# Spreading the running maxima of four recurrent heads over the partitions: by DMAs that read one row 128 times in place of selector products and copies

## The chip, the cores and the metric

One core of one Trainium2 chip runs the whole program in one launch. The metric is device time in microseconds (us) of that core; before, three runs gave 3002.44, 3003.31 and 3006.01, median 3003.31. A core has five engines with their own instruction streams (TensorE or PE, VectorE or DVE, ScalarE or ACT, GpSimd or POOL, SyncE or SP) that meet only at semaphores, an on-chip memory of 128 partitions (SBUF), eight accumulator banks (PSUM) and 16 DMA engines. Here SP issues most loads, and ACT issues some.

## The reference, cut to what matters

The model runs two transformer layers over 512 tokens of width 1024 and then a second block, whose middle is a bidirectional gated recurrence (mLSTM) of 4 heads over 256 context and 512 latent tokens. The part that the change touches is the stabiliser of that recurrence. In the reference:

```
b = jnp.cumsum(jax.nn.log_sigmoid(f_pre).reshape(bsz, nh, nc, CHUNK), axis=-1)
dmat = jnp.where(mask, b[..., :, None] - b[..., None, :] + ip[..., None, :], -jnp.inf)
inter = b + m_in[..., None]
m_t = jnp.maximum(jnp.max(dmat, axis=-1), inter)
s = jnp.einsum('bhctk,bhcsk->bhcts', q, k) * jnp.exp(dmat - m_t[..., None])
```

The kernel doesn't work by chunk states. For a head h and a direction d it computes, for each block of 128 keys s, the weight exp(ip_s - b_s - M_t) for all 512 latent queries t, where M_t is the running maximum over keys of ip - b up to t. M is one row of 512 numbers for each (h, d). In the weights the keys lie on the partitions and the queries in the free dimension, so the row M must stand in all 128 partitions: that copy is `maximum(h, d)`, 128x512 numbers of fp32.

## The kernel before, in words

Every large product is made of three fp32r products (`mm3`, L454 to L457: high by high, low by high, high by low), each over a stationary 128x128 block and up to 512 columns. Weights come from DRAM in chunks of 512 KB (eight 128x128 blocks) into four stage slots, which SP loads in order (`load`, L2827: chunk i waits until chunk i-4 is split); ACT makes the high part (`weights`, L1233 to L1257), DVE the low part (L1888), and PE uses the chunk. The order of work on each engine is written out by hand, function by function; nothing is reordered at run time.

The part around the change, in PE's order:

- Gates: DVE makes the running sums and maxima of the eight gate rows by scans; row 32d+h of `T0[:, 256:768]` is M for (h, d). `gates_last` (L2472) ends with the semaphore name "scans". `SEL` is a constant of 36x1024 that SP loads into `TAB` (L2857): block 4d+h has ones in row 32d+h alone.
- The `pu` products (L1014 to L1027), eight steps k of four `mm3` each, two steps to a weight chunk; after k = 1 PE transposes the gates (`columns_of_gates`, L998), after k = 4 and 6 it runs `running_max(0, d)` (L1010): a product of the selector block and T0 into the bank `STAT`. ACT copies the bank to `maximum(0, d)` (L1713).
- `output_gate(3)` (its weights are the chunk after those of `pu`), then the pool means (`poolm` chunks, L1116), the first q and k, and the loop over the heads.
- The loop over h = 0..3 and over key blocks c = 0..5: PE makes the scores; ACT makes the exponents from `maximum(h, d)` (`exponents`, L1750; on the diagonal block DVE L2547 and ACT L1754); DVE multiplies (L2557); ACT takes the high part (L1276), POOL the low part (L2706); PE multiplies with the values and sums (`sums`, L1080 to L1082). `running_max(h+1, d)` stands in c = 2 and 3 of head h, on PE behind the scores of the next block and on ACT behind `weigh(h, c)`. At a head's end ACT runs `exponents(h+1, 0)` and then `denominators(h)` (L1769), for which PE's transposes (L1091) and DVE (L2565) wait; the normalisation of head h is done during head h+1.

Of the kernel before, what the change touches and what calls it, by code (L numbers as in the profile page):

```python
# [189 lines left out]

def program(nc, ws, wm, xT, cT, params, cond, consts, sel_d, out, plan):
    dry, chunks, upto = plan.dry, plan.chunks, plan.upto
    signals = {}
    ctx = ExitStack()
    with ctx:
        def signal(name, step=1):
            signals[name] = Signal(name, ctx.enter_context(nc.semaphore(f"s_{name}")), plan, step)
            return signals[name]
# [10 lines left out]
        landed = [signal(f"ws{i}", 16) for i in range(NS)]  # L209
        modl = [signal(f"md{i}", 16) for i in range(6)]  # L210
        x_in = [signal(f"x{t}", 16) for t in range(DT)]
        par_in, cond_in, idn_in, dft_in, c_in, rope_in, sel_in, mask_in, stored = (
# [30 lines left out]
        ROPE = [TAB[:, 896:1408], TAB[:, 1408:1920]]  # L243
        SEL = TAB[0:GATE_ROWS, 0:1024]
        TRI = [TAB[:, 1024:1152], TAB[:, 1152:1280]]
# [93 lines left out]
        def maximum(h, d):  # L339
            return Z[:, 4 + 2 * (h % 2) + d, :]  # L340

        def folded(g):


            a = 16 * S if g % 2 == 0 else 0
            return GHf[:, a:a + 514], GLf[:, a:a + 514]
# [70 lines left out]
        SCORE_OF = {n: name for name, n in SCORES.items()}  # L417
        def maximum_bank(h, d):

            return PS[2 * (h % 2) + d] if h else STAT  # L420


# [9 lines left out]
        def tensor(e):  # L432
# [568 lines left out]

            def running_max(h, d):
                if h == 0:
                    stat_free()
                elif h == 1:
                    banks.wait(pe, 2 + d)
                else:
                    pe.wait_ge(dv, "nrm", h - 2, d)
                a = (d * 4 + h) * 128
                done(e.matmul(maximum_bank(h, d)[:, :], SEL[:, a:a + 128], T0[:, 256:768], start=True, stop=True), ("mx", h, d))  # L1010
                if h == 0:
                    stat["free"] = (ev, ("mx", h, d))

            pu = [take_bank(("pu", c), lo, "pu", c) for c in range(4)]  # L1014
            for k in range(8):
                wh, wl = block(*[("w_in2", 0, k * 128, 1552 + q * 128) for q in range(4)])
                for c in range(4):
                    inst = mm3(pu[c][:, :], HH[:, k, c * 128:c * 128 + 128], HL[:, k, c * 128:c * 128 + 128], wh, wl, k == 0, k == 7)
                if k == 7:
                    ended(inst, ("pu",))  # L1020
                elif cur["used"] == 8:
                    ended(inst)
                if k == 1:
                    columns_of_gates()
                elif k in (4, 6):
                    pe.wait_ge(sel_in, "sel")
                    running_max(0, k // 2 - 2)  # L1027

# [34 lines left out]
            def sums(h, c):  # L1063
                if c == 0:
                    if h == 0:
                        for d in range(2):
                            banks.wait(pe, d)
                        pe.wait_ge(modv, "m", len(MODS) - 1)
                    else:

                        pe.wait_ge(lo, "qk", h, 0)
                        pe.wait_ge(ev, "mx", h, 1)
                        pe.wait_ge(ev, "den", h - 1)
                for d in range(2):
                    a, b = spans(c, d)
                    es = WEIGHED[h, c, d] % 4
                    eh, el = GH[:, 14 + es, 0:b - a], GL[:, 14 + es, 0:b - a]
                    va = GH[:, 6 + c, h * 128:h * 128 + 128], GL[:, 6 + c, h * 128:h * 128 + 128]
                    pe.wait_ge(plo, "e", h, c, d)
                    mm3(PS[2 * (h % 2) + d][:, a:b], *va, eh, el, c == 0, c == 5)  # L1080
                    e.matmul(DEN[0:2, a:b], ROW[:, d, :], eh, start=c == 0 and d == 0, stop=False, skip_group_check=True)
                    inst = e.matmul(DEN[0:2, a:b], ROW[:, d, :], el, start=False, stop=c == 5 and d == 1,  # L1082
                                    skip_group_check=True)
                    done(inst, ("sum", h, c, d))
# [83 lines left out]
            for h in range(NH):  # L1168
                more = h + 1 < NH
                for c in range(5):  # L1170
                    scores(h, c + 1)
                    if h == 0 and c == 1:
                        pool_out(3)
                    if c < 2 and h:
                        normalize(h - 1, c)
                    elif 2 <= c < 4 and more:
                        running_max(h + 1, c - 2)
                    if c >= 2 and not more:
                        early(*beside[2 * c - 4:2 * c - 2])
                    if c:  # L1180
                        sums(h, c - 1)
                    if c == 3 and h:
                        head_sums(h - 1)
                    elif c == 4 and h:
                        rms_last(("hn", h - 1), S, dv, "hn1", h - 1)
                if more:
                    pe.wait_ge(ev, "mx", h + 1, 0)
                    q_and_k(h + 1, 0, maximum_bank(h + 1, 0))
                else:
                    early(*beside[6:8])  # L1190
                sums(h, 4)
                if more:
                    q_and_k(h + 1, 1, score_bank("qk", h + 1, 1))
                    q_and_k(h + 1, 2, score_bank("qk", h + 1, 2))
                else:
                    early(*beside[8:10])
                sums(h, 5)
                if more:
                    scores(h + 1, 0)
                else:  # L1200
                    early(*beside[10:12])
                denominators(h)
# [26 lines left out]
        def scalar(e):  # L1229
# [471 lines left out]
            for c in range(2):  # L1701
                high(GH[:, 6 + c, :], bank("v2", c)[:, :], "v2", c)

            weights(("tr",))
            act.wait_ge(dv, "gct")
            act.wait_ge(mm, "tr")
            e.activation(GC[:, 6:10, :].rearrange("p a b -> p (a b)"), STAT[:, 216:360], ACT.Exp,
                         scale=-1.0).then_inc(ev.sem, ev.up(("fc",)))

            def running_max(h, d):  # L1710
                act.wait_ge(mm, "mx", h, d)
                act.wait_ge(padd, "out+", ("ao", 0, 0), 6)
                e.activation(maximum(h, d), maximum_bank(h, d)[:, :], ACT.Copy).then_inc(ev.sem, ev.up(("mx", h, d)))  # L1713

# [18 lines left out]
            def exponents(h, c):  # L1733
                for d in range(2):
# [10 lines left out]
                    if before:  # L1745
                        act.wait_ge(signals[before[0]], *before[1])
                    act.wait_ge(ev, "mx", h, d)
                    if rest.stop > rest.start:
# [46 lines left out]

            for d in range(2):
                weights(("mx", 0, d))
                running_max(0, d)
            exponents(0, 0)
# [16 lines left out]
            for h in range(NH):  # L1816
                more = h + 1 < NH
                for c in range(5):
                    exponents(h, c + 1)
                    weigh(h, c)  # L1820
                    if c < 2 and h:
                        normalize(h - 1, c)
                    elif 2 <= c < 4 and more:
                        running_max(h + 1, c - 2)
# [8 lines left out]
                if more:  # L1833
                    q_and_k(h + 1, 0, maximum_bank(h + 1, 0))
                    q_and_k(h + 1, 1, score_bank("qk", h + 1, 1))
                    q_and_k(h + 1, 2, score_bank("qk", h + 1, 2))
                    exponents(h + 1, 0)
# [26 lines left out]
        def vector(e):  # L1864
# [671 lines left out]
            def exponents(h, c):  # L2536

                for d in range(2):
# [3 lines left out]
                    if c >= 2:  # L2542
                        dd = slice(0, 128) if d == 0 else slice(n - 128, n)
                        dve.wait_ge(ev, "mx", h, d)
                        dve.wait_ge(dv, "gct")
# [81 lines left out]
            for h in range(NH):  # L2627
# [19 lines left out]
                if more:  # L2647
                    q_and_k(h + 1, 0, maximum_bank(h + 1, 0))
                    q_and_k(h + 1, 1, score_bank("qk", h + 1, 1))
                    q_and_k(h + 1, 2, score_bank("qk", h + 1, 2))  # L2650
                    exponents(h + 1, 0)
# [165 lines left out]
        def sync(e):  # L2817
# [32 lines left out]
            for i in range(6, nch):  # L2850
# [4 lines left out]
                if i == select_at:  # L2855
                    sp.wait_ge(lo, "h", ("an", 1, 1), 7)
                    e.dma_start(SEL, sel_d).then_inc(sel_in.sem, sel_in.up(("sel",)))  # L2857
                    e.dma_start(TAB[:, 1024:1280], consts[:, 4992:5248]).then_inc(sel_in.sem, sel_in.up(("sel",)))
# [55 lines left out]
def constants():  # L2914
# [17 lines left out]
    c[:, 5120:5248] = np.where(i[:, None] >= i[None, :], 0, 1e4)  # L2932
    sel = np.zeros((GATE_ROWS, 8, 128), np.float32)
    for d2 in range(2):
        for h in range(4):
            sel[32 * d2 + h, d2 * 4 + h] = 1
    j = np.arange(512)
# [11 lines left out]
    for g, win in enumerate((2, 4, 8, 16)):  # L2949
# [9 lines left out]
        c[:, 5248 + 512 * g:5760 + 512 * g] = 1 / count  # L2959
    return c, sel.reshape(GATE_ROWS, 1024), dft.astype(np.float32), poolm.astype(np.float32)  # L2960

# [82 lines left out]
```

## Time and profile before

| | us |
|---|---|
| median of three runs | 3003.31 (3002.44 to 3006.01) |
| profiled execution, its span | 3002.8 |
| PE busy | 2963.0 (99%) |
| DVE busy | 1785.7 (59%) |
| ACT busy | 1128.1 (38%) |
| POOL busy | 226.3 (8%) |

The page gives no other time for the profiled execution than its span. Times in the rows are from the span's start. A matmul's duration overlaps the next one's: a 512-column product lasts 0.39 us, and the next starts 0.23 us after it; time on PE is therefore counted from start to start. A mark such as [0.40 <-POOL GL L2706] is idle time ahead of a row and what ended it.

### The profile page before, as it was taken

Reading aid. Unit: us, or ns where it says so; the run is one execution under the profiler, and the core shown is the slowest. Engines: PE = TensorE matmul, PEld = TensorE weight load, DVE = VectorE, ACT = ScalarE, POOL = GpSimd, SP = SyncE. Lnnn points to the kernel's source line nnn. Section 1 sums busy time; section 2 is a strip of 40 time slices with the busy share of each in tenths; the row PEclk is TensorE's granted clock in tenths of the full one; section 3 lists DMA queues with packets and bytes.
Section 4 is the critical chain, followed back from the end, with each engine's and each line's share of the span. In section 5 each row is a group of like instructions: output and inputs, shape, how many; then the busy total and the mean of one; then the engine's idle time right before and its main releaser. Section 6 shows DMA issues by size and latency. Waiting matters only on the chain. (4 is left out here: it accounts for less than half of the span.)

```text
span 3002.8 us, 36219 instructions
## 1 busy us (share of the span) xinstructions
PE 2963.0 (99%) x14767; PEld 2491.8 (83%) x14767; DVE 1785.7 (59%) x2589; ACT 1128.1 (38%) x1690; POOL 226.3 (8%) x184
## 2 busy tenths in 40 slices
PE   7999999999999999999999999999999999999999
PEld 6888888888888888888888899888899866788887
DVE  7767666765867667677757656323357656443233
ACT  4433332433424333333434344222235556332222
POOL 0300000000001201100000011000011014100000
PEclk9999999999999999999999999999999999999999
DMA  7454355344433433344443344232235230123221
GB/s 287 152 183 141 126 182 196 126 141 136 144 126 114 152 120 121 109 148 140 148 136 137 133 134 162 98 99 93 97 126 173 91 126 8 57 92 98 98 97 65
DMA packets 107781, 383.83 MB, mean 128 GB/s; under 512 B 11964, under 2 KB 13372, under 8 KB 107616
## 3 DMA queue, kind: packets, MB, share of 16 engines
q1 hardware_dynamic: 83856, 296.51, 29.5%
q10 hardware_dynamic: 23760, 85.01, 8.7%
q8 instruction: 117, 1.92, 0.3%
q14 instruction: 48, 0.39, 0.0%
HBM read 379.37 MB, written 2.10 MB: 127 GB/s over the span
## 5 line engine op out<-in xcount | busy, mean ns | idle before, releaser
L1888 DVE TENSOR_TENSOR WL<-stage,WH 128x1024 fp32r<-128x1024 f32 x508 | 630.5, 1243 | 563.1 <-ACT WH L1256 562.9
L455 PE MATMUL ps<-HH,WH 128*128 128x512 f32 x2184 | 853.4, 391 | 0.3 <-DVE WL L1888 0.3
L456 PE MATMUL ps<-HL,WH 128*128 128x512 f32 x2184 | 850.2, 389 | 0.0
L457 PE MATMUL ps<-HH,WL 128*128 128x512 f32 x2184 | 849.9, 389 | 0.0
L1256 ACT ACTIVATE WH<-stage 128x1024 fp32r<-128x1024 f32 x512 | 537.6, 1053 | 440.7 <-PE ps L457 429.1
L455 PE MATMUL ps<-GH,WH 128*128 128x512 f32 (+2 forms) x1649 | 572.0, 347 | 2.6 <-DVE SCR L2557 1.8
L456 PE MATMUL ps<-GL,WH 128*128 128x512 f32 (+2 forms) x1649 | 569.0, 345 | 0.0
L457 PE MATMUL ps<-GH,WL 128*128 128x512 f32 (+2 forms) x1649 | 569.0, 345 | 0.0
L457 PEld LDWEIGHTS ps<-HH,WL 128*128 128x128 f32 x2184 | 409.9, 188 | 85.8
L455 PEld LDWEIGHTS ps<-HH,WH 128*128 128x128 f32 x2184 | 410.1, 188 | 83.6 <-issue 1.4
L456 PEld LDWEIGHTS ps<-HL,WH 128*128 128x128 f32 x2184 | 410.2, 188 | 82.7
L455 PEld LDWEIGHTS ps<-GH,WH 128*128 128x128 f32 x1649 | 312.0, 189 | 45.3 <-DVE SCR L2557 2.7
L456 PEld LDWEIGHTS ps<-GL,WH 128*128 128x128 f32 x1649 | 312.2, 189 | 39.3
L457 PEld LDWEIGHTS ps<-GH,WL 128*128 128x128 f32 x1649 | 312.1, 189 | 37.6
L1276 ACT ACTIVATE GH<-SCR 128x512 fp32r<-128x512 f32 (+5 forms) x310 | 164.9, 549 | 430.6 <-DVE SCR L2125 125.3
L1915 DVE CUSTOM_DVE_ANT_0 MST<-MST,CB,PAR 128x1024 f32<-128x1024 f32 x158 | 205.1, 1298 | 3.8 <-DMA MST<-wm 2.7
L2706 POOL TENSOR_TENSOR GL<-SCR,GH 128x512 fp32r<-128x512 f32 (+3 forms) x102 | 116.1, 1157 | 739.7 <-ACT GH L1276 739.5
L2684 POOL TENSOR_TENSOR V<-V,HM 128x4 f32<-128x4 f32 (+1 forms) x26 | 31.9, 1228 | 1796.3 <-DVE V L1959 1796.3
L1930 DVE TENSOR_TENSOR GL<-SCR,GH 128x512 fp32r<-128x512 f32 (+1 forms) x192 | 121.6, 641 | 58.3 <-ACT GH L1276 56.5
L1495 ACT ACTIVATE SCR<-ps,PAR 128x512 f32<-128x512 f32 x88 | 68.3, 779 | 159.8 <-PE ps L457 158.9
L2372 DVE TENSOR_TENSOR SCR<-ps,SCR 128x512 f32<-128x512 f32 (+1 forms) x66 | 39.7, 601 | 119.4 <-PE ps L457 112.9
L1594 ACT ACTIVATE SCR<-ps 128x512 f32<-128x512 f32 (+1 forms) x66 | 34.7, 526 | 188.4 <-PE ps L457 182.6
(265 smaller groups left out, 2905.1 us busy)
## 6 DMA issues: line engine op xcount, KB each, us to landing
stage<-ws SPq DMA_DIRECT2D x535, 512.0 KB, 3.3
MST<-wm ACTq DMA_DIRECT2D x154, 512.0 KB, 3.3
Z<-wm SPq DMA_DIRECT2D x10, 512.0 KB, 7.9
TAB<-consts ACTq DMA_DIRECT2D x7, 448.0 KB, 3.5
MST<-wm SPq DMA_DIRECT2D x6, 512.0 KB, 7.2
out<-X SPq DMA_DIRECT2D x8, 256.0 KB, 2.2
X<-xT SPq DMA_DIRECT2D x4, 256.0 KB, 5.2
X<-xT ACTq DMA_DIRECT2D x4, 256.0 KB, 5.5
```

Of the source, the lines that this page charges most:

```text
L455: e.matmul(o, wh, mh, start=start, stop=False, **more)
L456: e.matmul(o, wh, ml, start=False, stop=False, **more)
L457: return e.matmul(o, wl, mh, start=False, stop=stop, **more)
L1256: e.activation(wh, src, ACT.Copy).then_inc(whi.sem, whi.up(("w", i)))
L1276: e.activation(dst, src, ACT.Identity if "bias" in more else ACT.Copy, **more).then_inc(hi.sem, hi.up(name))
L1495: e.activation(T, bank("up", l, c)[:, :], ACT.Identity, scale=par("cw", (l * 3 + 1) * 44 + c), bias=par("cb", l * 44 + c)).then_inc(ev.sem ...
L1594: e.activation(T, bank("sa", who, half, jj)[:, 0:n], ACT.Silu).then_inc(ev.sem, ev.up(("sa", who, half, jj)))
L1888: e.tensor_tensor(wl, src, wh.bitcast(F32), ALU.subtract).then_inc(wlo.sem, wlo.up(("w", i)))
L1915: e.tensor_tensor_reduce(out=products, in0=a, in1=b, scale=1.0, scalar=res if i else bias, op0=ALU.mult, op1=ALU.add, accum_out=res).then_inc(
L1930: e.tensor_tensor(dst, src, high_part.bitcast(F32), ALU.subtract).then_inc(lo.sem, lo.up(name))
L2372: made(e.tensor_tensor(T, bank("sb", who, half, jj)[:, 0:n], T, ALU.mult), "sb", who, half, jj)
L2706: e.tensor_tensor(dst, src, high_part.bitcast(F32), ALU.subtract).then_inc(plo.sem, plo.up(name))
```

## The change

The selector constant, its load, the eight selector products on PE and the eight copies on ACT go. In their place ACT issues eight DMAs, each reading one row of `T0` (one partition, 512 numbers) with a partition step of zero 128 times and writing all 128 partitions of `maximum(h, d)`. Each of four semaphores serves one buffer. The four DMAs of heads 0 and 1 are issued together behind `weights(("tr",))`, when "scans" is done; those of heads 2 and 3 stand where ACT's copies stood (c = 2 and 3 of heads 1 and 2). `exponents(0, 0)` on ACT moves ahead of the weights of `output_gate(3)`, and the readers wait for the DMA.

```diff
+        max_in = [signal(f"mx{i}", 16) for i in range(4)]
...
+        def max_landed(h, d):
+
+            return max_in[2 * (h % 2) + d], "mx", h, d
...
-            def running_max(h, d):
-                if h == 0:
-                    stat_free()
-                elif h == 1:
+            def sums_bank(h, d):
+
+                if h == 1:
                     banks.wait(pe, 2 + d)
-                else:
+                elif h > 1:
                     pe.wait_ge(dv, "nrm", h - 2, d)
-                a = (d * 4 + h) * 128
-                done(e.matmul(maximum_bank(h, d)[:, :], SEL[:, a:a + 128], T0[:, 256:768], start=True, stop=True), ("mx", h, d))
-                if h == 0:
-                    stat["free"] = (ev, ("mx", h, d))
+                return PS[2 * (h % 2) + d]
...
-                elif k in (4, 6):
-                    pe.wait_ge(sel_in, "sel")
-                    running_max(0, k // 2 - 2)
...
-                        pe.wait_ge(ev, "mx", h, 1)
+                        sums_bank(h, 1)
...
-                    elif 2 <= c < 4 and more:
-                        running_max(h + 1, c - 2)
...
+            def running_max(h, d):
+                if h < 2:
+                    act.wait_ge(dv, "scans")
+                    act.wait_ge(padd, "out+", ("ao", 0, 0), 6)
+                else:
+                    act.wait_ge(ev, "e", h - 2, 5, d)
+                    act.wait_ge(dv, "g1", h - 2, 5, d)
+                s = max_in[2 * (h % 2) + d]
+                row = T0[32 * d + h:32 * d + h + 1, 256:768]
+                e.dma_start(maximum(h, d), row.unsqueeze(1).to_broadcast([1, 128, S])).then_inc(s.sem, s.up(("mx", h, d)))
+
             weights(("tr",))
+            for h in range(2):
+                for d in range(2):
+                    running_max(h, d)
             act.wait_ge(dv, "gct")
...
-            def running_max(h, d):
-                act.wait_ge(mm, "mx", h, d)
-                act.wait_ge(padd, "out+", ("ao", 0, 0), 6)
-                e.activation(maximum(h, d), maximum_bank(h, d)[:, :], ACT.Copy).then_inc(ev.sem, ev.up(("mx", h, d)))
...
-                    act.wait_ge(ev, "mx", h, d)
+                    act.wait_ge(*max_landed(h, d))
...
-            for d in range(2):
-                weights(("mx", 0, d))
-                running_max(0, d)
+            weights(("tr",), ahead=3)
             exponents(0, 0)
             weights(("pu",))
...
-                    elif 2 <= c < 4 and more:
+                    elif 2 <= c < 4 and h and more:
                         running_max(h + 1, c - 2)
...
-                        dve.wait_ge(ev, "mx", h, d)
+                        dve.wait_ge(*max_landed(h, d))
...
-                    e.dma_start(SEL, sel_d).then_inc(sel_in.sem, sel_in.up(("sel",)))
```

## Rows read from the trace of the kernel before

**Rows 1.** The page: the span, and busy time of each engine.
```profile
span 3002.8 us, 36219 instructions
PE 2963.0 (99%) x14767; PEld 2491.8 (83%) x14767; DVE 1785.7 (59%) x2589; ACT 1128.1 (38%) x1690; POOL 226.3 (8%) x184
```
**Rows 2.** The lines that go: ns min/median/max, first and last start us.
```profile
L1010 PE MATMUL ps<-GT,TAB x16: 589/641/693, 2425.9 to 2520.9; 36*128 36x512 f32 x16
...
L1713 ACT ACTIVATE Z<-ps x8: 573/578/599, 2427.1 to 2523.6; 128x512 f32<-128x512 f32 x8
```
**Rows 3.** Chain of waits from `pu` to the pool means: start us, us, what.
```profile
2425.97 1.05 PE ps L1010 x2
...
2442.69 1.06 ACT WH L1256
...
2443.77 4.20 DMA stage<-ws
```
**Rows 4.** PE in order of time around one selector product, and output_gate(3)'s first.
```profile
2425.59 0.39 PE L457 MATMUL ps<-WH,HL 128*128 128x512 f32 x1
2425.90 1.12 PE L1010 MATMUL ps<-GT,TAB 36*128 36x512 f32 x2
2426.96 0.50 PE L455 MATMUL ps<-WH,HH 128*128 128x512 f32 x1
...
2436.56 0.39 PE L455 MATMUL ps<-HH,WH 128*128 128x512 f32 x1
```
**Rows 5.** PE in order of time in head 2, c = 2.
```profile
2520.36 1.12 PE L1010 MATMUL ps<-GT,TAB 36*128 36x512 f32 x2
2521.89 0.50 PE L455 MATMUL ps<-GH 128*128 128x512 f32 x1 [0.40 <-POOL GL L2706]
```
**Rows 6.** Chain of waits in head 1, c = 2, and at its end.
```profile
2493.24 1.39 POOL GL L2706
...
2508.41 0.41 PE ps L1091 x4
```
**Rows 7.** All engines in order of time: ACT in head 1.
```profile
2493.27 0.57 ACT L1713 ACTIVATE Z<-ps 128x512 f32<-128x512 f32 x1
...
2496.43 0.58 ACT L1713 ACTIVATE Z<-ps 128x512 f32<-128x512 f32 x1
...
2506.00 1.34 ACT L1750 ACTIVATE SCR<-Z,GC 128x512 f32<-128x512 f32 x2
...
2507.76 0.59 ACT L1769 ACTIVATE GT<-ps 2x512 f32<-2x512 f32 x1 [0.42 <-PE ps L1082]
```
**Rows 8.** ACT in order of time ahead of the heads.
```profile
2411.24 1.06 ACT L1256 ACTIVATE WH<-stage 128x1024 fp32r<-128x1024 f32 x1
2417.65 1.28 ACT L1707 ACT_TABLE_LOAD   x1 [5.35 <-PE ps L998]
```
**Rows 9.** DVE in order of time: the scans' last copy, and output_gate(3)'s low weights.
```profile
2409.29 0.42 DVE L2478 COPY GT<-GT 4x512 f32<-4x512 f32 x1
...
2424.39 1.23 DVE L1888 TENSOR_TENSOR WL<-stage,WH 128x1024 fp32r<-128x1024 f32 x1 [2.94 <-ACT WH L1256]
```
**Rows 10.** DMA issues on ACT's queue: ns of the issue.
```profile
L1430 ACTq DMA_DIRECT2D TAB<-consts x7: 334/334/335, 215.4 to 1199.1; - x7
```
**Rows 11.** The page's DMA issues: KB each, us from issue to landing.
```profile
stage<-ws SPq DMA_DIRECT2D x535, 512.0 KB, 3.3
out<-X SPq DMA_DIRECT2D x8, 256.0 KB, 2.2
```
**Rows 12.** DMA busy tenths and GB/s in 40 slices of 2440 to 2450 us.
```profile
DMA  0000068499975000002969898999999799999999
GB/s 0 0 0 0 0 66 180 131 410 410 393 311 197 0 0 0 0 0 33 246 180 328 279 426 344 426 360 410 426 442 361 246 360 410 410 426 377 393 426 377
```
**Rows 13.** Engines by stretch: us, busy (x) of PE, PEld, DVE, ACT, POOL, PEclk, DMA share, GB/s.
```profile
2457.50:2460.30 2.80, 1.74 (x6) 1.13 (x7) 1.60 (x4) 2.24 (x4) 2.52 (x2) 1.00 0.00 0
2460.30:2463.70 3.40, 3.40 (x10) 2.00 (x9) 2.13 (x5) 2.82 (x6) 1.73 (x2) 0.51 0.00 0
```

More of the change, by code:

```diff
@@ L188, in drain, with program @@
             self.advance()
-def program(nc, ws, wm, xT, cT, params, cond, consts, sel_d, out, plan):
+def program(nc, ws, wm, xT, cT, params, cond, consts, out, plan):
     dry, chunks, upto = plan.dry, plan.chunks, plan.upto
@@ L243, in program @@
         ROPE = [TAB[:, 896:1408], TAB[:, 1408:1920]]
-        SEL = TAB[0:GATE_ROWS, 0:1024]
         TRI = [TAB[:, 1024:1152], TAB[:, 1152:1280]]
@@ L417, in program @@
         SCORE_OF = {n: name for name, n in SCORES.items()}
-        def maximum_bank(h, d):
-            return PS[2 * (h % 2) + d] if h else STAT
         WEIGHED = {}
@@ L1186, in tensor @@
                 if more:
-                    pe.wait_ge(ev, "mx", h + 1, 0)
-                    q_and_k(h + 1, 0, maximum_bank(h + 1, 0))
+                    q_and_k(h + 1, 0, sums_bank(h + 1, 0))
                 else:
@@ L1833, in scalar @@
                 if more:
-                    q_and_k(h + 1, 0, maximum_bank(h + 1, 0))
+                    q_and_k(h + 1, 0, PS[2 * ((h + 1) % 2)])
                     q_and_k(h + 1, 1, score_bank("qk", h + 1, 1))
@@ L2647, in vector @@
                 if more:
-                    q_and_k(h + 1, 0, maximum_bank(h + 1, 0))
+                    q_and_k(h + 1, 0, PS[2 * ((h + 1) % 2)])
                     q_and_k(h + 1, 1, score_bank("qk", h + 1, 1))
@@ L2932, in constants @@
     c[:, 5120:5248] = np.where(i[:, None] >= i[None, :], 0, 1e4)
[L2933 to L2936, printed above, removed]
     j = np.arange(512)
@@ L2959, in constants @@
         c[:, 5248 + 512 * g:5760 + 512 * g] = 1 / count
-    return c, sel.reshape(GATE_ROWS, 1024), dft.astype(np.float32), poolm.astype(np.float32)
+    return c, dft.astype(np.float32), poolm.astype(np.float32)
 def kernel(x, c, norm1_g, norm2_g, ada_w, ada_b, w_in, w_fourier, w_ret, w_out, ffn_up, conv_w, conv_b,
@@ L2970 @@
     A = lambda a: np.ascontiguousarray(a)
-    consts, sel, dft, poolm = constants()
+    consts, dft, poolm = constants()
     gate = np.zeros((1024, 128), np.float32)
@@ L3015, in build @@
         ins = {"ws": (n, 128, 1024), "wm": (len(MODS), 128, 1024), "cond": (128, 1024), "xT": (8, 128, S), "cT": (8, 128, C), "params": (128, NP),
-               "consts": consts.shape, "sel": sel.shape}
+               "consts": consts.shape}
         t = {k: nc.dram_tensor(k, v, F32, kind="ExternalInput").ap() for k, v in ins.items()}
         out = nc.dram_tensor("out", (8, 128, S), F32, kind="ExternalOutput").ap()
-        program(nc, t["ws"], t["wm"], t["xT"], t["cT"], t["params"], t["cond"], t["consts"], t["sel"], out, plan)
+        program(nc, t["ws"], t["wm"], t["xT"], t["cT"], t["params"], t["cond"], t["consts"], out, plan)
         return nc
@@ L3039 @@
     arrays = {"ws": ws, "wm": wm, "xT": A(A(x)[0].T).reshape(8, 128, S), "cT": A(A(ctx_2)[0].T).reshape(8, 128, C),
-              "params": P, "cond": A(every(c)), "consts": consts, "sel": sel}
+              "params": P, "cond": A(every(c)), "consts": consts}
     r = run_bass_kernel_spmd(nc, [arrays], core_ids=[0])
```

## Prediction

> **What bounds the kernel now.** I read the page first: PE is busy 99% of a span of 3002.8 us, so nothing is won except time that PE spends in work or in a wait [rows 1]. The question is whether the selector products stand where PE itself sets the pace, and the list of a line's instructions says where they are: eight products in sixteen passes, all between 2425.9 and 2521 us, and eight copies beside them [rows 2]. Then the chain of waits over that stretch. From the `pu` products to the end of `output_gate(3)` the chain runs on PE alone, and both products of head 0 lie in it, one of them in the row shown (the other is the same, 6.7 us later) [rows 3]. There a selector product costs its full time. In the head loop the chain is another one: ACT's high part, POOL's low part, DVE's weighing and short stretches of PE in turn [rows 6]. There PE has gaps, and the order of time shows one: behind the selector product of head 2 PE waits 0.40 us for POOL's low part all the same [rows 5]. So two of the eight products are on the path and six are beside it.
>
> **The change part by part.**
>
> *Products of head 0.* A 512-column product normally starts 0.23 us after the one before. Around the first selector product the starts are 2425.59 and 2426.96, 1.37 apart, so it costs 1.14 us [rows 4]; two cost 2.3. Everything behind them is released by PE's end: the chain goes from PE to ACT's split of a weight chunk, to a load, to the pool means [rows 3], and all of it moves with PE. Gain by itself: 2.3 us.
>
> *Products of heads 1 to 3.* Six of the same, 6.8 us on PE. POOL's low part, not PE, releases the next sum [rows 5, 6], so they are worth nothing; if every one of them counted it would be 6.8 more.
>
> *Copies.* Eight of 0.58 us on ACT [rows 2]. The two of head 0 stand where ACT was waiting for PE. Each of the others stands between a high part and the exponents of the next block; what follows waits for DVE or POOL, so 0, at best their 0.58 each, 3.5 in all.
>
> *DMA issues.* An issue holds ACT 0.334 us [rows 10]. Four are issued from 2412.3 on, when ACT's weight split ends and "scans" is long done (2409.7) [rows 8, 9]: they take 1.3 us of an idle time of 5.35, no cost. Four more take 0.33 in place of 0.58 each in the loop, no cost.
>
> *Selector load.* One of the constants' loads on SP goes, long before its use; nothing waited for it.
>
> *The DMAs themselves.* No row of before reads SBUF from one partition, so I bound it. Low end: a store of the same 256 KB that reads all 128 partitions lands 2.2 us after its issue [rows 11]. High end: all 16 engines ask the same partition. The highest slice of the DMA view is 442 GB/s, 27.6 for one of 16 engines [rows 12]. If one partition hands out no more than one engine's stream, 262,144 bytes take 9.5 us. The store's own data takes 262,144 / 442e3 = 0.6 us, so 1.6 of its 2.2 is fixed: one DMA lands after 11.1 us, and since they stand in one queue, the second of a pair lands 9.5 us behind the first. I take this end. The nearest row by size is the store, but its source spreads over every partition, which is just what this DMA doesn't do; the row nearest in kind is the stream of one engine.
>
> The Trainium skill speaks against the change here ("SBUF — State Buffer", section "Door 1: The DMA port swizzle"): a partition is reached over one of 16 ports of about 27.2 GB/s, and partitions p and p+32, so both rows of a head, share one. By that a row's 128 reads would take an estimated 9.6 us. No row of before shows a port at its limit.
>
> *What the wait then costs at head 0.* The four DMAs are issued from 2412.3. The first lands at 2423.4, the second at 2412.3 + 1.6 + 19.0 = 2432.9. ACT stands in `exponents(0, 0)` until then, and behind it in ACT's queue is the high part of `output_gate(3)`'s weights. From 2432.9: exponent 0.67 (half of the 1.34 for two [rows 7]), high part 1.06 [rows 8], low part on DVE 1.23 [rows 9], ready at 2435.9. PE wants it at 2436.56 - 2.3 = 2434.3 [rows 4], and waits 1.6. Left of the gain: 2.3 - 1.6 = 0.7 us. Head 1's rows land by 2452, well ahead of head 1's first exponents (about 2478).
>
> *What it costs at heads 2 and 3.* The issues stand where ACT's copies stood, at 2493.27 and 2496.43 in head 1 [rows 7]. The second row lands at 2493.27 + 1.6 + 19.0 = 2513.9. ACT wants it for the second half of `exponents(2, 0)` at 2506.00 + 0.67 = 2506.67, so it is 7.2 us late. Queued behind it on ACT is `denominators(1)`, which had 0.42 us of slack [rows 7]; PE's transposes wait for that, then DVE, the normalisation and the sums, and those are on the chain [rows 6]. Cost 7.2 - 0.4 = 6.8 us. Head 3 repeats head 2 some 27.2 us later with the same distances (the copy of head 2's c = 3 starts at 2523.6 [rows 2]): 6.8 again. Sum 13.6. Heads 0 and 1 have no such wait.
>
> *Loads beside the row DMAs.* From 2412 to 2452 the weight loads run on the same 16 engines as the row DMAs, and one load of that time, from 2443.77, is on the chain with 4.20 us where a load has 3.3 in the median [rows 3, 11]. If the loads weren't hindered: 0. If each engine took one packet of a load and one 2 KB row in turn, a load's eight packets per engine would wait for eight rows of 16 x 2048 / 27.6e3 = 1.19 us each, 9.5 us, and the chunk of the second pool mean, wanted at about 2443, would come at 2451: 8 us. Four loads or so lie in that time, and all but one had slack. Between 0 and 8 I take 2: that row shows a load lengthened by 0.9 in a crowd, and the crowd is now about twice as long.
>
> **Sum.** -0.7 + 13.6 + 2.0 = 14.9 us on a profiled span of 3002.8, which is 0.5 under the median of the runs. From the median: 3003.3 + 14.9 = 3018.2 us.
>
> **The rivals.**
>
> A. *The rows spread as fast as the store does.* Then nothing is late, the gain of head 0 is whole, and the time is 3003.3 - 2.3 = 3001. For it: the data path is wide, 442 GB/s in a slice [rows 12], and 256 KB is little. Against it: sixteen engines read one partition. Its point of decision: twice the service time and 1.6 must fit between the first issue and the need, 2506.67 - 2493.27 = 13.4 us, so a row must be through in 5.9 us (44 GB/s). This is the side of no loss.
>
> B. *The loads wait their turn behind the rows.* As priced above, 8 us at the pool means in place of 2: 3003.3 - 0.7 + 13.6 + 8 = 3024. Each stall may also leave PE at the lower clock for a while: after the gaps near 2457 to 2460 the granted clock is 0.51 of full speed, the lower of its two levels (1.2 GHz), for 3.4 us [rows 13], which would add up to 1.7 us for each of two or three stalls.
>
> The Trainium skill ("DMA: Bandwidth & Descriptors", section "Queues, rings and completion order") says that an engine goes round between its queues packet by packet. That is what B needs; the trace of before has hardly two queues busy at once in this stretch and shows neither.
>
> C. *The products of the loop count after all.* If PE's 6.8 us in heads 0 to 2 were on the path and the rows landed in time, 3003.3 - 2.3 - 6.8 = 2994. Against it: the wait on POOL right behind a product [rows 5].
>
> **Chances.** Forecast (rows served one after another, loads little hindered) 0.42, B 0.21, A 0.28, C 0.04, a row slower than one engine's stream (over 3030) 0.05. The range reaches from A to above B: 2999 to 3030. The forecast's own range is 3012 to 3022. What a measurement can tell from no change is 0.2%, 6 us. Faster by more holds C only and a little of A: 0.05. The same holds A, and rows of 6 to 8 us: 0.28. Slower holds the forecast, B and the rest: 0.67.
>
> **What would show it.** In the profile after: DMAs on ACT's queue of 256 KB with some 11 us to landing for the first of a pair and 17 to 20 for the second (A: 2 to 4 for each); ACT idle some 7 us ahead of the second L1750 of `exponents(2, 0)` and of `exponents(3, 0)`, released by a DMA; PE idle for about as long around its transposes, and head periods of 34 where they were 27; a PE wait of 1 to 2 us ahead of `output_gate(3)` for DVE's L1888. Loads with landings near 10 us between 2412 and 2452 would speak for B. The forecast is wrong if a row's landing is under 7 us, or if the head periods don't grow.

## The result, and the profile after

The changed kernel takes 3028.45 us (median of four runs, 3026.17 to 3030.61) where the kernel before takes 3003.34; the ratio is 1.0083, 95% interval 1.007 to 1.0095. It is 25 us slower. The forecast was 3018.2 with 2999 to 3030.

The page of the profile after: PE is busy 2965.6 us (2963.0 before) in a span 25.7 us longer, the row DMAs (`Z<-GT`) land in 17.3 us in the median, and they are in the chain that ended last.

```profile
span 3028.5 us, 36193 instructions
PE 2965.6 (98%) x14751; PEld 2499.6 (83%) x14751; DVE 1782.5 (59%) x2589; ACT 1124.4 (37%) x1682; POOL 227.1 (7%) x184
...
PE ps L455 4%; PE ps L457 4%; PE ps L456 4%; DMA Z<-GT 1%; PE ps L572 0%; PE ps L850 0%; PE ps L496 0%; DVE SCR L2321 0%; PE ps L497 0%; PE ps L500 0%; PE ps L838 0%; PE ps L547 0%; POOL GL L2703 0%; POOL X L2694 0%; PE ps L842 0%
...
Z<-GT ACTq DMA_DIRECT2D x8, 256.0 KB, 17.3
```

**Where the time went.** `denominators(h)` on ACT (L1769 before, L1768 after) marks each head's end. Before, the four start at 2479.81, 2507.76, 2534.95 and 2563.45; after, at 2490.81, 2525.10, 2559.10 and 2588.13. So 11.0 us are lost up to the end of head 0, 6.3 more in head 1, 6.8 in head 2 and 0.5 in head 3; the last 1.0 of the 25.7 comes behind head 3.

The two losses in the middle are the waits that were forecast. ACT in order of time, from the issue of head 2's rows (L1703) to its exponents (L1749), and the same wait for head 3's:

```profile
2503.26 0.48 ACTq L1703 DMA_DIRECT2D Z<-GT  x1
...
2507.04 0.48 ACTq L1703 DMA_DIRECT2D Z<-GT  x1
...
2516.99 0.73 ACT L1749 ACTIVATE SCR<-Z,GC 128x512 f32<-128x512 f32 x1
2524.48 0.72 ACT L1749 ACTIVATE SCR<-Z,GC 128x512 f32<-128x512 f32 x1 [6.76 <-DMA Z<-GT]
2525.10 0.57 ACT L1768 ACTIVATE GT<-ps 2x512 f32<-2x512 f32 x1
...
2558.48 0.72 ACT L1749 ACTIVATE SCR<-Z,GC 128x512 f32<-128x512 f32 x1 [6.74 <-DMA Z<-GT]
2559.10 0.57 ACT L1768 ACTIVATE GT<-ps 2x512 f32<-2x512 f32 x1
```

The first row of the pair is there in time, the second is not: 2524.48 - 2503.26 = 21.2 us from the first issue to the second landing. This answers to [rows 7], where the exponents of both directions ran without a gap.

The 11.0 us ahead of it show on ACT and PE together. ACT in order of time, from the last two of the first four issues:

```profile
2411.31 16.94 ACTq L1703 DMA_DIRECT2D Z<-GT  x2
2428.34 1.28 ACT L1711 ACT_TABLE_LOAD   x1 [16.24 <-issue]
...
2432.14 0.73 ACT L1749 ACTIVATE SCR<-Z,GC 128x512 f32<-128x512 f32 x1 [0.67 <-DMA Z<-GT]
...
2441.38 1.06 ACT L1246 ACTIVATE WH<-stage 128x1024 fp32r<-128x1024 f32 x1 [7.57 <-DMA stage<-ws]
...
2452.45 1.06 ACT L1246 ACTIVATE WH<-stage 128x1024 fp32r<-128x1024 f32 x1 [6.87 <-DMA stage<-ws]
```

ACT stands 16.2 us in the issue of the third and fourth row DMA (before, the same table load stood behind 5.35 us of idle [rows 8]), and then twice some 7 us for a weight load. The issues of the third and fourth end at 2418.2 and 2428.3, ten us apart. PE, in order of time, waits for the chunks that come late:

```profile
2432.18 0.50 PE L455 MATMUL ps<-WH,HH 128*128 128x512 f32 x1 [3.71 <-DVE WL L1885]
2451.57 0.80 PE L1109 MATMUL ps<-WH,GH 128*128 128x512 f32 x1 [4.87 <-DVE WH L1876]
```

And after each long wait PE works for some us at the lower of its two clock levels (1.2 GHz). PE by stretch (us, busy (x), granted clock, DMA share, GB/s), behind the wait of 4.87 us and behind head 2's:

```profile
2452.00:2456.00 4.00, 3.99 (x10) 0.50 1.03 418
2524.00:2528.00 4.00, 2.27 (x9) 0.50 0.00 0
2528.00:2532.00 4.00, 4.00 (x18) 0.50 0.00 0
```

**What a row DMA does.** In 2505 to 2521 us nothing but head 2's rows moves. The DMA view (busy tenths, GB/s, in 40 slices) shows engines that are busy most of the time (0.5 to 0.9) and move 15 to 41 GB/s, 27 in the mean, where the loads reached 442 [rows 12]:

```profile
DMA  9959869869689589689889888988986986985985
GB/s 36 31 15 36 26 20 36 26 20 36 20 26 36 15 26 36 20 26 31 26 26 31 26 26 26 31 26 26 31 26 20 36 26 20 36 26 15 41 26 15
```

That is about what one of 16 engines moved at the 442 (27.6), now shared by all 16: 262,144 / 27e3 = 9.7 us for a row.

### The profile page after: what moved, and what is told of

It is laid out like the page before. It is cut to its first block and busy times, and to the rows that moved or that the text cites. A ratio compares the mean times of both kernels' runs of the same rounds, so it can differ in the third digit from the quotient of the medians.

```text
span 3028.5 us, 36193 instructions
## 1 busy us (share of the span) xinstructions
PE 2965.6 (98%) x14751; PEld 2499.6 (83%) x14751; DVE 1782.5 (59%) x2589; ACT 1124.4 (37%) x1682; POOL 227.1 (7%) x184
## 6 DMA issues: line engine op xcount, KB each, us to landing
Z<-GT ACTq DMA_DIRECT2D x8, 256.0 KB, 17.3
```

## The experiments

Times are medians; each ratio is against runs of the kernel before on the same chip. The label in each heading is used below.

**e1, heads 2 and 3 earlier.** After `weigh(h, 5)` of head h, ACT issues head h+2's rows; the place at c = 2 and 3 goes.

```diff
-                    elif 2 <= c < 4 and h and more:
-                        running_max(h + 1, c - 2)
...
                 weigh(h, 5)
+                if h + 2 < NH:
+                    for d in range(2):
+                        running_max(h + 2, d)
```

> Only the place of the row DMAs of heads 2 and 3 is changed: they are issued at the end of heads 0 and 1, some 29 us before their use. Theory (one row served after another, 9.6 us each, so a pair takes 21 us to land): both waits of ACT for a row, 6.8 us each in the profile after, go, and the time is 3028.5 - 13.4 = 3015. Rival (the rows' traffic itself, or the issue on ACT, costs in the loop wherever it stands): a part of the 13.4 comes back, 3020 or more.

3017.56 us, ratio 1.0048 (1.0035 to 1.006), between the 3015 and the 3020 of the two theories. In the profiled execution, at 3015.55 the fastest of the five, neither wait for a row is left in the loop, and heads 1 and 2 take 28.1 and 27.4 us where the changed kernel has 34.3 and 34.0 and the kernel before 28.0 and 27.2. The waits were worth 10.9 us by the medians and 12.8 between the heads' ends; there the traffic of the rows costs next to nothing, and what made the other four executions slower isn't known.

**e2, head 1 later.** Head 1's pair is issued just before the loop.

```diff
             weights(("tr",))
-            for h in range(2):
-                for d in range(2):
-                    running_max(h, d)
+            for d in range(2):
+                running_max(0, d)
...
             pool_mean(3)
+            for d in range(2):
+                running_max(1, d)
             for h in range(NH):
```

> The two row DMAs of head 1 are issued just before the loop over the heads, not together with head 0's. Theory (four rows in flight hold ACT in the issue of the third and fourth for 16 us and hold back the weight loads until about 2452 us): with two rows ACT isn't held in an issue, the loads are free from about 2433 us on, and of the 11 us lost up to the end of head 0 some 2 to 3 are left: 3020. Head 1's rows then land some 21 us after about 2457 us, just in time. Rival (head 0's own pair does the harm): 3027 to 3029.

3014.76 us, ratio 1.0037 (1.0025 to 1.005), a greater gain than expected. Head 0 ends at 2479.47, level with the kernel before (2479.81): ACT issues without a stop, and in place of PE's waits of 3.71 and 4.87 us stand these:

```profile
2434.61 0.47 PE L455 MATMUL ps<-HH,WH 128*128 128x512 f32 x1 [0.55 <-DVE WL L1886]
2451.43 0.50 PE L1109 MATMUL ps<-WH,GH 128*128 128x512 f32 x1 [1.20 <-DVE WH L1877]
```

PE's granted clock stays at 1.00 up to the end of head 0. All 11 us came from having head 1's two rows in flight beside head 0's and the loads, with what follows from it.

**e3, both moves** (the two diffs above together).

> Both moves of the last two kernels. If the two costs are separate they add: 3028.5 - 13.4 - 8 = 3007. If they share a cause, less is won than the two alone show.

3005.01 us, ratio 1.0006 (0.9997 to 1.0015). Alone the moves win 10.9 and 13.7, together 23.4: two separate costs, as far as the noise lets one tell. Repaired in this way the idea comes out even with the kernel before, not ahead. No wait for a row is left in heads 1 and 2, yet they take 31.2 and 30.5 us: the granted clock is 0.50 from 2496 to 2500 us and 0.53 from 2524 to 2528 (more on this at e4).

**e10, head 1's pair behind the first exponents.** To tell the held issue from the loads: the pair is issued when head 0's has landed.

```diff
             weights(("tr",))
-            for h in range(2):
-                for d in range(2):
-                    running_max(h, d)
+            for d in range(2):
+                running_max(0, d)
...
             weights(("tr",), ahead=3)
             exponents(0, 0)
+            for d in range(2):
+                running_max(1, d)
```

> As the changed kernel, but head 1's two row DMAs are issued behind exponents(0, 0), when head 0's two have landed: never more than two are in flight, so ACT isn't held in an issue, but rows are still in flight beside the loads of the pool means until about 2452 us. If the loads behind the rows cost the time (rival B of the prediction), PE still waits 4 to 5 us for the chunk of the second pool mean and head 0 ends 5 to 8 us late: about 3022 to 3025. If only the held issue did, head 0 ends as in the kernel before and the time is that of the kernel with head 1's pair just before the loop, 3014.8.

3028.38 us, ratio 1.0087 (1.0073 to 1.0101), as slow as the changed kernel and above the 3022 to 3025 expected, though the issues behind one another take 0.5 us each and hold nobody. Head 0 ends at 2491.44. PE in order of time shows one long wait in place of two (for the gate's weights it waits 1.23 us):

```profile
2453.35 0.80 PE L1109 MATMUL ps<-WH,GH 128*128 128x512 f32 x1 [10.11 <-DVE WH L1877]
```

And the DMA view of 2430 to 2455 shows why (slices of 0.63 us):

```profile
DMA  8999999988888888889695969696979895899999
GB/s 292 419 420 419 420 416 243 29 26 26 26 26 26 26 26 26 26 26 33 20 36 23 75 69 95 62 102 62 95 66 98 66 85 56 275 420 419 419 419 419
```

Loads alone run at 420 GB/s; rows alone at 26; and while both are there, at some 80, about three times 26: for each 2 KB of a row, by this ratio, an engine moves 4 KB of a load, which is one partition's part of a chunk. That is rival B of the prediction, and by it the loads behind the rows are enough for the whole 11 us, without a held issue. The trace agrees with the rule of the Trainium skill that the forecast set beside B ("DMA: Bandwidth & Descriptors", section "Queues, rings and completion order").

**e7, head 1's pair from POOL.** Issued at about 2409 us, with a semaphore of its own.

```diff
-            for h in range(2):
-                for d in range(2):
-                    running_max(h, d)
+            for d in range(2):
+                running_max(0, d)
...
+            pool.wait_ge(dv, "scans")
+            pool.wait_ge(padd, "out+", ("ao", 0, 0), 6)
+            for d in range(2):
+                row = T0[32 * d + 1:32 * d + 2, 256:768]
+                e.dma_start(maximum(1, d), row.unsqueeze(1).to_broadcast([1, 128, S])).then_inc(pool_in[d].sem, pool_in[d].up(("mx", 1, d)))
```

> As the changed kernel, but head 1's two row DMAs are issued by POOL, which is idle then, at the same time as head 0's by ACT. ACT isn't held in an issue; the rows in flight are the same. If the 16 us that ACT stood in the issue are the cause of the 11 us lost before head 1, most of it comes back: 3028.5 - 8 = 3020. If the loads are held back by the rows on the DMA engines, whoever issues them, it stays: 3026 to 3029.

3037.96 us, ratio 1.0112 (1.0098 to 1.0126): above both expectations. With two queues the pairs share the slow read in turn, and head 0's second row, needed first, lands after 40 us; ACT waits 11.9 and 18.2 us for the two and PE 20.0 for the gate's weights. Another queue doesn't make the reads faster, and takes away the order in which they were wanted. So this run doesn't separate the held issue from the loads; e10 does.

**e8 and e9, four partitions in place of one.** Each DMA reads four partitions, each 32 times: 0 to 3 in e8, and 0, 4, 8, 12 in e9. The maxima are then other rows than the reference's; only size, place and queue stay.

```diff
-                row = T0[32 * d + h:32 * d + h + 1, 256:768]
-                e.dma_start(maximum(h, d), row.unsqueeze(1).to_broadcast([1, 128, S])).then_inc(s.sem, s.up(("mx", h, d)))
+                rows = T0[0:4:1, 256:768]    # e9: T0[0:16:4, 256:768]
+                e.dma_start(maximum(h, d), rows.unsqueeze(1).to_broadcast([4, 32, S])).then_inc(s.sem, s.up(("mx", h, d)))
```

> Each of the eight DMAs reads partitions 0, 1, 2, 3, each 32 times, in place of one row 128 times (so the maxima are other rows and the output isn't the reference's); sizes, places and queue stay. If the limit is what one partition gives, four partitions give four times as much: landing about 4 to 5 us, time near 3004. If these four share a port (Trainium skill, "SBUF — State Buffer", section "Door 1: The DMA port swizzle"), the landing stays at 11 to 12 us for the first of a pair and the time near 3028.

> As the last kernel, but each DMA reads partitions 0, 4, 8, 12, each 32 times. If the limit belongs to a port that partitions 0 to 3 share, these four partitions are on four ports and a DMA lands in 4 to 5 us, time near 3004, where the last kernel stays slow. If the number of DMA engines that take part sets the rate, both kernels have the same landing.

e8: 3035.51 us, ratio 1.0105 (1.0087 to 1.0124). e9: 3003.76 us, ratio 0.9995 (0.9984 to 1.0007). The DMA views, of 2508 to 2524 us in e8 and of 2490 to 2498 us in e9:

```profile
DMA  1222212122121221212212122121212122221322
GB/s 26 20 20 31 26 20 26 20 31 26 20 26 20 31 26 20 26 20 31 26 20 26 20 31 26 20 26 20 31 20 26 20 26 26 26 26 20 67 26 41
```

```profile
DMA  0012222222222220000002222222222222110000
GB/s 0 0 72 102 102 102 102 102 102 92 102 92 113 92 113 21 0 0 0 0 0 92 102 102 102 102 102 102 92 92 92 82 113 82 41 51 0 0 0 0
```

While rows move, both keep at most about a quarter of the 16 engines busy (mostly 0.1 to 0.2). Four partitions side by side give 24 GB/s, no more than one; four that are four apart give 102, four times as much. So what is slow is neither the repetition nor the single partition but something that partitions 0 to 3 share, and it gives 24 to 27 GB/s. This fits the port of the Trainium skill ("SBUF — State Buffer", section "Door 1: The DMA port swizzle", 27.2 GB/s each); that p and p+32 share one was not tried alone.

e8 is 7 us slower than the changed kernel, where it was expected level: head 0 ends 3.6 us later, and heads 1 and 2 each take 1.9 more, for a rate of 24 in place of 27. e9 came out as expected, though its head 1 takes 32.7 us: the granted clock is 0.50 from 2492 to 2500 us.

**e4, the rows by way of DRAM.** Two DMAs store the eight rows to a DRAM tensor behind the scans, and the spreads read that.

```diff
+            act.wait_ge(dv, "scans")
+            for d in range(2):
+                e.dma_start(rows[4 * d:4 * d + 4, :], T0[32 * d:32 * d + 4, 256:768]).then_inc(rows_out.sem, rows_out.up(("rows",)))
+            act.wait_ge(rows_out, "rows")
...
-                row = T0[32 * d + h:32 * d + h + 1, 256:768]
-                e.dma_start(maximum(h, d), row.unsqueeze(1).to_broadcast([1, 128, S])).then_inc(s.sem, s.up(("mx", h, d)))
+                row = rows[4 * d + h:4 * d + h + 1, :]
+                e.dma_start(maximum(h, d), row.to_broadcast([128, S])).then_inc(s.sem, s.up(("mx", h, d)))
```

> The eight rows are stored to DRAM once, by two DMAs behind the scans, and each maximum is spread from the row in DRAM instead of from the row's one partition; places, queue, sizes and waits stay. Theory (the one partition that all engines read is what is slow): a spread lands in 2.5 to 5 us, nothing waits, the two selector products of head 0 are saved on PE's path: 3001 (2.3 under before). Rival (a row read 128 times is slow wherever it lies): landings stay above 10 us and the time near 3025.

3004.32 us, ratio 1.0003 (0.9994 to 1.0012), where 3001 was expected. The first spread is issued 2.0 us behind the store. The spreads land in 3.0 to 9.5 us, median 4.9, and no engine waits for one. Head 0 ends at 2477.88, 1.9 us ahead of before, as the forecast's 2.3 had it. But the next two ends are 2506.46 and 2537.53: head 2 takes 31.1 us in place of 27.2, and the gain is gone; over the whole profiled span e4 is level with before (3002.8 both). The clock shows where. PE by stretch over head 2 in e4, where before it was 1.00:

```profile
2504.00:2532.00 28.00, 25.17 (x111) 0.82 0.06 20
```

It fell behind these two waits, the second of which is 0.40 in the kernel before [rows 5]:

```profile
2518.90 0.51 PE L457 MATMUL ps<-GH 128*128 128x512 f32 x1 [0.45 <-DVE SCR L2560]
2521.31 0.50 PE L457 MATMUL ps<-GH 128*128 128x512 f32 x1 [1.44 <-POOL GL L2709]
```

The same waits don't always bring it down. e1 has no products in the loop either and waits in head 2 just as long, and its clock stays at 1.00:

```profile
2534.25 0.50 PE L455 MATMUL ps<-GH 128*128 128x512 f32 x1 [1.43 <-POOL GL L2704]
2520.00:2548.00 28.00, 23.64 (x127) 1.00 0.52 17
```

Heads 1 and 2 of e1, e3, e4, e6 and e9, ten in all, have this wait of 1.4 us. Behind five of them the clock fell (e3 both heads, e4 and e6 head 2, e9 head 1), behind five it didn't. In the kernel before, e5 and e11, where something stands in the gap, it fell at this place in none of six. Each kernel was profiled in one execution only.

**e6, no loop products and nothing in their place.** The kernel before, with the six products and copies of heads 1 to 3 taken out; `maximum(h, d)` is `Z[:, 4 + d, :]` for all heads, so heads 1 to 3 use the maxima of head 0.

```diff
-                    elif 2 <= c < 4 and more:
-                        running_max(h + 1, c - 2)
```

> The kernel before without the selector products and copies of heads 1 to 3, and with no DMA in their place: heads 1 to 3 use the maxima of head 0, so the output isn't the reference's. Theory (they are beside the path, but keep PE's clock): 3003 + 2 to 5 = 3005 to 3008, with slices of granted clock near 0.5 in heads 1 or 2. Rival (they are simply hidden): 3003. Rival C of the prediction (they are on the path): 2996.5.

3005.46 us, ratio 1.0006 (0.9997 to 1.0015): by time alone no change can be told, and 2996.5 is excluded, rival C with it. The profiled execution, at 3009.55 the slowest of the eleven, shows what can happen: head 2 takes 32.5 us (2509.16 to 2541.66), with 8 us in it at about half clock.

```profile
2524.00:2528.00 4.00, 4.00 (x17) 0.52 0.00 0
2528.00:2532.00 4.00, 4.00 (x14) 0.50 0.00 0
```

**e5, e4 with fillers.** Where the selector product stood in the loop, PE runs five products of ones, 1.25 us in the trace where the selector product has 1.12.

```diff
+            def keep_busy(h, d):
+                P = sums_bank(h, d)
+                for _ in range(5):
+                    e.matmul(P[:, :], ONR[:, 0:1].to_broadcast([128, 128]), ONR[:, 0:1].to_broadcast([128, S]), start=True, stop=True)
...
+                    elif 2 <= c < 4 and more:
+                        keep_busy(h + 1, c - 2)
```

> The kernel with the rows spread from DRAM, and in the loop over the heads PE runs five products of ones (512 columns each, about 1.1 us) where the selector product of the kernel before stood; their result is overwritten. Theory (the loop's selector products, though beside the path, filled gaps of PE; without them the granted clock fell to 0.5 in heads 1 and 2, which ate the gain): the clock stays near 1 there, a head takes 27.2 us again, and the time is 2.3 us under before: 3001. Rival (the rows' own DMAs or their later landing cost the time): 3004 as without the fillers.

3001.31 us, ratio 0.9991 (0.9982 to 0.9999), 2.2 us under before, as expected. The same stretch of PE, now with more work in it:

```profile
2504.00:2532.00 28.00, 25.44 (x138) 1.00 0.06 20
```

Head 2 takes 27.2 us again. With work whose result nobody reads the kernel is 3.0 us faster than e4 by the medians of eleven runs each, on two chips whose kernel before differs by 0.3; the two intervals of the ratios just overlap.

**e11, more fillers.** Four more of them behind `scores(0, 1)` and `scores(0, 2)`, where the clock fell in the kernel before [rows 13] and in e4, e5 and e6, though not in e2, e3 and e9: "in every kernel so far" is too much.

```diff
+                    if h == 0 and c < 2:
+                        stat_free()
+                        for _ in range(4):
+                            e.matmul(STAT[:, :], ONR[:, 0:1].to_broadcast([128, 128]), ONR[:, 0:1].to_broadcast([128, S]), start=True, stop=True)
```

> The kernel with rows from DRAM and fillers in the loop, with four more products of ones behind scores(0, 1) and scores(0, 2), where PE waits in every kernel so far and the granted clock falls to 0.51 for 3.4 us. If these gaps caused that fall, it goes, and up to 1.7 us with it: 3000, about the limit of what can be told. If the fillers only delay, 3002 to 3003.

3001.18 us, ratio 0.9993 (0.9984 to 1.0002). The clock is at 1.00 from 2456 to 2464 us and head 0 ends 0.9 us earlier than in e5 (2476.02 against 2476.87), but in head 1 it is 0.84 and 0.73 from 2500 to 2508, where e5 has 1.00, and that head takes 28.8 us in place of 27.9. Over the whole time the two can't be told apart.

## Why the prediction was right, and where it was short

*What bounds, and which products are on the path: right for head 0.* Two products were worth 2.3 us by the sum. With rows that land in time head 0 ends 1.9 us earlier (e4), and 2.9 where fillers keep the loop's products in place (e5).

*The price of a row: right.* Forecast 9.5 us for each after a fixed 1.6; measured 9.7 (27 GB/s) and a first landing of 11.9. The choice of the high end over the store's 2.2 us decided the forecast. Its reason was right in kind, but the sum laid the limit on the one partition: e8 shows that partitions 0 to 3 together give no more.

*The wait for head 0's rows: about right, once alone.* Forecast was a PE wait of 1.6 us and 0.7 us left of the gain; in e2, where only head 0's pair is in flight, the wait is 0.55 and head 0 ends 0.3 us ahead of before. In the changed kernel, with the held issue, it is 3.71.

*Heads 2 and 3: right.* Forecast 6.8 us each, 13.6 in all; measured 6.3 and 6.8 between the heads' ends.

*DMA issues, "no cost": wrong.* An issue of a row takes 0.48 to 0.6 us, not 0.33, which is harmless; but the third and fourth of four rows held ACT 16.2 us, which split a chunk late and made PE wait 3.7 us. Nothing in the rows of before showed an issue that was held.

*Loads beside the row DMAs: the term that was mis-sized.* The forecast took 2 us from a range of 0 to 8, by the row of a load lengthened by 0.9 in a crowd. With -0.7 for head 0 that made +1.3 up to head 0's end; it was +11.0. That row was the wrong neighbour: there the loads crowded among themselves at 420 GB/s, here each of their packets stood behind a row that comes at 26 GB/s. The mechanism had been written down as rival B with a price of 8, in sum 3024, and e2 and e10 show it at work. The time came out 4.5 us above even B. Part of this is the lower clock behind each wait, which B named and didn't put in its sum. An estimate from PE's stretches of 1 us between 2424 and the end of head 0 (busy time times what is missing of the clock) puts it at 6.3 us where before had 1.7, so some 4.6 of the 11.0; PE's waits for the two late chunks are the greater part of the rest (3.71 and 4.87 us). How much belongs to the held issue wasn't separated, since e2 removes it with the rest and e10 trades two waits for one. That the range held the time is owed to its width, which reached past B; the forecast's own number was 10 us short, nearly all of it ahead of head 0's end, in this term and in the held issue.

*Loop products "worth nothing": probably wrong in sign, with no effect on the forecast here.* They fill PE's gaps. Behind the one of head 2 in rows 5 PE had 0.40 us left to wait; without it it waits 1.44 us in e4. Where the clock fell behind that wait the head took 3 to 5 us more (e3, e4, e6, e9); with fillers it didn't fall there (e5, e11). It doesn't fall each time (e1), and by time alone e6 can't be told from before, so the sign rests on e4 against e5. Rival A would hardly have reached its 3001 either: with rows that land in time and no fillers the medians are 3004.3 (e4) and 3003.8 (e9), though e9's interval still holds 3001.

## What to carry to other kernels

Before a DMA is to spread one partition over all, divide its bytes by what one partition gives (26 GB/s here), not by what the DMA engines move together, and count every other DMA that runs beside it as waiting its turn. If the row must be spread by DMA, store it to DRAM first and spread it from there: 3 to 9.5 us, behind 2 us for the store, in place of 12 to 33. And ahead of taking work off TensorE, look at the gaps that it fills and at the granted clock behind them: six fillers of 1.25 us made the kernel some 3 us faster here (e4 against e5).

## What the runs showed of the hardware

- One partition read 128 times gave a DMA 26 to 27 GB/s, partitions 0 to 3 gave 24 and partitions 0, 4, 8, 12 gave 102, the last two with a quarter of the engines busy at most (changed kernel and e10; e8; e9).
- ACT could issue two such DMAs of 128 reads without a stop; in the issue of the third it stood 6.9 us and in that of the fourth 10.0, about the 9.7 us of a row. With four partitions the three issues behind the first took 9.2 us in all at 24 GB/s (e8) and 3.6 at 102 (e9).
- TensorE's granted clock fell to 0.50 (1.2 GHz) behind waits of 0.45 and 1.4 us in head 2 of e4; behind the same waits it stayed at 1.00 in e1, in head 1 of e4 and in head 2 of e9. In the kernel before and in e5, where 0.40 and less stood in place of the 1.4, it stayed at 1.00.
- Weight loads alone moved 420 GB/s; beside a row DMA on the other queue, loads and rows together moved some 80 (e10).
